# A two-model forward pass of fp32 on one core: S5 preparation in 25 smaller steps, residuals loaded by tile, packed matmuls in SSD and S5, and VectorE's stage steps ahead of the low part of the weights

## The chip, the cores and the metric

The kernel runs on one core of one Trainium2 chip. The metric is the device time of one execution in microseconds (us), as the median of several runs; smaller is better. A profiled execution is one run with the hardware profiler on, and its own time is given beside its span.

## What is computed

Two models follow each other on one sequence of 512 tokens and width 2048, everything in fp32. The first has a layer of gated linear attention (4 heads) and forgetting attention (8 heads), and a layer with an S5 state space model and a gated linear unit. The second has two equal layers with three branches each: SSD (Mamba-2 in chunks of 128, 16 heads of 64), a conformer convolution with 31 taps, and differential attention (4 heads). Around each stand RMS norms, a wide input projection and an output projection onto the residual. Cut to what the change touches:

```python
# S5: x_t = Lbar x_{t-1} + Bbar u_t ; y_t = Re(C x_t) + D u_t, 128 groups of 16 channels, 64 complex states each
bu = einsum('gpc,blgc->blgp', bb, uf); x = associative_scan(...); y = einsum('gcp,blgp->blgc', c, x) + d * uf
# SSD, one head h, chunks of L = 128:
a_cs = jnp.cumsum(a, axis=-1)
decay_in = segsum_exp(a_cs)                       # exp(a_cs[l] - a_cs[s]) for s <= l
y_diag = jnp.einsum("bcgls,bcgjls,bcsgjp->bclgjp", cb, decay_in, xdt)
y = (y_diag + y_off + d_skip * x) * silu(z)
x = x + jnp.einsum("bse,ed->bsd", y_all, w_out[l])
```

## The kernel before, in words

**Projections.** All dense products are cut into 528 units (`UNITS`). A unit is one load of 512 KB of weights and 24 matmuls of 128x128 by 128x512: each fp32 product is made of three fp32r products, high by high, low by high and high by low part (`unit_pe`, L541 and L542). Eight units (or six and two, for output projections that are split into `x_in`/`x_normed` and `x_part`) make a pass, which fills four PSUM banks. The last unit of a pass goes bank by bank, so that the banks are emptied (`evac_dve`, `evac_act`) while it still runs; the first unit of the next pass waits for each bank to be free.

**Slots.** Each engine runs through the same 528 slots in order. In slot t TensorE does unit t and then the steps of that slot that belong to the small computations between the projections ("stages": GLA, forgetting attention, S5, SSD, convolution, attention). Their steps are Python generators, one `yield` for each slot, placed by hand in tables (`stage`, `place`); `take(t)` issues those of slot t. Four PSUM banks (`mid`) are theirs.

**Weights.** The SyncE queue (SP) loads unit t+5 in slot t (`weights_sp`) once VectorE (DVE) has made the low part of unit t+2 (a ring of three buffers). In slot t ScalarE (ACT) rounds unit t+2 to its high part (`weights_act`, L394), once unit t-1 is used up, and DVE then subtracts to get the low part (`weights_dve`, L467).

**Activations.** Sixteen tiles of 128x512 for each projection phase are split into high and low parts too ("conversions", two tiles a slot as a rule, at slots listed in `conversions()`): a load (`convert_sp`, four buffers), ACT's high part, and for some phases squares for the norm that GpSimd (POOL) adds up (`convert_act`, `add_pool`), and DVE's low part (`convert_dve`, L525 and L528). They lie in slots -1 to 4, 106 to 111, 140 to 147, 202 to 209, 234 to 239 with 242 and 243, 266 to 271 with 274 and 275, 362 to 365 with 368 and 369, 396 to 403, 490 to 493 with 496 and 497, and one tile at a time in slots 117, 121, 125, 129, 213 and in the attention heads of the last two layers.

**The order on the two queues.** This is what the change turns on; VectorE (L2637 to L2648) and SP (L2572 to L2582), for each slot t:

```python
# vector
evac_dve(e, ENDS[t - 1])          # if slot t-1 ended a pass
weights_dve(e, t + AHEAD)         # low part of unit t+2
convert_dve(e, n)                 # conversions of slot t
take(t)                           # stage steps of slot t
# sync
store_sp(e, ENDS[t - 1]); take(t)
weights_sp(e, t + 5)              # waits for the low part of unit t+2
residual_sp(e, UNITS[t][0])       # in the first slot of a pass that adds a residual
convert_sp(e, n)                  # loads for the conversions of slot t+1
```

**Parts that the change touches.** `prep_dve` (L760 to L856) computes the S5 constants in 12 steps in slots 5 to 16. `sw_pe` (L988) makes the S5 kernels of 8 groups by matmuls with 16 output rows, into rows 0 to 15 of two banks, for each of 16 tiles in slots 76 to 138. In SSD each head h starts in slot 48+h of its layer (the layers start at slots 272 and 400): ACT spreads `a` (L1897), TensorE makes the cumulated sums with 4 fp32 matmuls (L1934), DVE and ACT form the exponentials (L1958, L1902, L1905), DVE multiplies (L1963), and two slots after its start TensorE makes y with 4 fp32 matmuls of 64 output rows (L1943), even heads in rows 0 to 63 of a bank and odd heads in rows 64 to 127. A residual of 4 tiles (1 MB) is loaded by one DMA (`residual_sp`, L347) in the first slot of its pass, after the pass before has been emptied, and added at L514.

Of the kernel before, what the change touches and what calls it, by code (L numbers as in the profile page):

```python
# [177 lines left out]
def build(nc, I, X):  # L178

    with ExitStack() as ctx:  # L180
# [38 lines left out]
        SMO = sb("small_out", [P, L])  # L219
        ONES = sb("ones", [P, P])  # L220
# [6 lines left out]
        ARENA_N = 19920  # L227
# [29 lines left out]
        out_stored, xr_in, zr_in = sem("out_stored"), sem("xr_in"), sem("zr_in")  # L257
# [38 lines left out]
        def x_source(q):  # L296

            w, l = PASSES[q], LAYER[q]
            if w.kind == "x_in":
                return I["x"][:, 4 * w.index:4 * w.index + 4, :], None  # L300
            if w.kind == "x_part":
                return XPART[l][4 * w.index:4 * w.index + 4].rearrange("k p n -> p k n"), q - 4
            src = XS[l - 1]
            return src[4 * w.index:4 * w.index + 4].rearrange("k p n -> p k n"), X_PASS[l - 1] + w.index
# [19 lines left out]
        def residual_sp(e, q):  # L324
# [8 lines left out]
            if PASSES[q].kind == "glu":  # L333
                i = PASSES[q].index
                stored(e, FIRST_GATE + i)
                e.dma_start(XR[:, :, :], FMD[1][4 * i:4 * i + 4].rearrange("k p n -> p k n")).then_inc(xr_in, 16)
                if i == 0:
                    for x in ZR_FREE:
                        e.wait_ge(*x)
                for k in range(4 * i, 4 * i + 4):  # L340
                    e.wait_ge(*mix_stored(3, k))
                e.dma_start(ZR[:, :, :], MX[3][4 * i:4 * i + 4].rearrange("k p n -> p k n")).then_inc(zr_in, 16)
                return
            src, by = x_source(q)
# [24 lines left out]
        def store_sp(e, q):  # L369
# [7 lines left out]
            for s in range(4):  # L377
# [9 lines left out]
                e.dma_start(dst, OUTB[:, s, :]).then_inc(out_stored, 16)  # L387

# [81 lines left out]
        def evac_dve(e, q):  # L470
# [26 lines left out]
            elif w.kind == "glu":  # L497
                e.wait_ge(xr_in, 16 * (XR_TURN[q] + 1))
                e.wait_ge(zr_in, 16 * (w.index + 1))
                for s in range(4):  # L500
                    e.wait_ge(*FREE[q, s])
# [3 lines left out]
            else:  # L505
                e.wait_ge(xr_in, 16 * (XR_TURN[q] + 1))
                if w.kind == "x_normed":
                    for s in range(4):
                        k = 4 * w.index + s
# [172 lines left out]
        def small_act(e, ph):  # L682
# [4 lines left out]
            if i == 1:  # L687
                e.wait_ge(*fx_p.at("lc", 7))
# [72 lines left out]
        def prep_dve(e):  # L761
# [72 lines left out]
            for d in range(8):  # L834
                if d % 3 == 0:
                    yield
# [1923 lines left out]
```

## Time and profile before

| | |
|---|---|
| median of 3 runs | 3628.29 us (3622.89 to 3630.3) |
| profiled execution, its own time | 3625.47 us |
| its span | 3623.7 us |
| granted TensorE clock, mean | 0.982 |
| TensorE busy | 3464.2 us, 96% |
| TensorE weight loads busy | 2770.9 us, 76% |
| VectorE busy | 2127.2 us, 59% |
| ScalarE busy | 1288.7 us, 36% |
| GpSimd busy | 150.4 us, 4% |
| DMA | 574.58 MB, mean 159 GB/s |

All times in the rows are us from the first instruction of the span, durations of groups of instructions in us or, where it is said, ns. Matmuls overlap: a 128x512 matmul is shown with about 390 ns although the next one starts earlier, so their starts, not their lengths, tell the pace.

### The profile page before, as it was taken

The page shows a single profiled execution, that of the slowest core. Times are in us where ns is not written, and L with a number is a line of the kernel's source. Part 1 is how long each engine was busy: PE and PEld are TensorE (multiplying, and loading weights), DVE is VectorE, ACT ScalarE, POOL GpSimd, SP SyncE. Part 2 cuts the span into 40 slices and gives each one's busy share as a digit, 9 for nine tenths or more (in the row PEclk, how much of TensorE's full clock was granted, in tenths as well). Part 3 has the DMA queues.
Part 4 walks back from the last instruction along what each step waited for, and adds up shares of the span by engine and source line. Part 5 has one row for each costly group of instructions (what it writes and reads, how often), then busy time and mean ns, then how long its engine had stood idle before and what let it go on. Part 6 is the DMA issues. An engine that isn't in the chain of part 4 may idle for free.

```text
span 3623.7 us, 42976 instructions
## 1 busy us (share of the span) xinstructions
PE 3464.2 (96%) x15890; PEld 2770.9 (76%) x15890; DVE 2127.2 (59%) x3122; ACT 1288.7 (36%) x2013; POOL 150.4 (4%) x100
## 2 busy tenths in 40 slices
PE   8899999999999999999989999998999999999899
PEld 6687887777777888788878876776777887677677
DVE  6755546677655645434244775566755476565774
ACT  4233324444332233423152224324423223532442
POOL 2000000000020000000050000000002000000000
PEclk9899999999999999999999999998999999999899
DMA  4233335566665555645443442344446343334445
GB/s 163 100 123 123 112 130 180 175 235 217 227 212 183 177 176 185 202 168 198 152 161 117 164 137 99 114 139 164 151 160 216 106 166 132 104 122 161 141 156 198
DMA packets 286129, 574.58 MB, mean 159 GB/s; under 512 B 61392, under 2 KB 101088, under 8 KB 285408
## 3 DMA queue, kind: packets, MB, share of 16 engines
q1 hardware_dynamic: 285920, 571.83, 47.0%
q8 instruction: 127, 2.08, 0.2%
q14 instruction: 82, 0.67, 0.1%
HBM read 440.65 MB, written 131.07 MB: 158 GB/s over the span
## 4 chain that ended last, share of the span: by engine, by line
PE 52%; issue 23%; DVE 13%; ACT 6%; DMA 3%; DVEq 2%; POOLq 1%; SPq 0%; ACTq 0%
PE bank L542 34%; PE bank L541 11%; DVE weights_low L467 3%; ACT weights_high L394 2%; DVE arena L1963 2%; ACT arena L1905 1%; POOLq L453 1%; DVE residual_in L2037 1%; DVE arena L1958 1%; DMA convert_in<-x 1%; PE bank L1076 1%; DVEq L2541 1%; ACT arena L1902 1%; DVE act_low L525 1%; PE bank L988 1%
## 5 line engine op out<-in xcount | busy, mean ns | idle before, releaser
L542 PE MATMUL bank<-act_high,weights_high 128*128 128x512 f32 x3584 | 1449.3, 404 | 77.1 <-DVE stream_out L514 34.7
L542 PE MATMUL bank<-act_low,weights_high 128*128 128x512 f32 x3584 | 1416.8, 395 | 0.0
L467 DVE TENSOR_TENSOR weights_low<-weights_raw,weights_high 128x1024 fp32r<-128x1024 f32 x528 | 656.9, 1244 | 1122.0 <-ACT weights_high L394 1119.4
L394 ACT ACTIVATE weights_high<-weights_raw 128x1024 fp32r<-128x1024 f32 x528 | 558.1, 1057 | 1517.7 <-PE bank L542 1256.4
L542 PE MATMUL bank<-act_high,weights_low 128*128 128x512 f32 x3584 | 962.8, 389 | 0.0
L542 PEld LDWEIGHTS bank<-act_high,weights_high 128*128 128x128 f32 x3584 | 686.1, 191 | 248.0 <-issue 54.4
L542 PEld LDWEIGHTS bank<-act_low,weights_high 128*128 128x128 f32 x3584 | 685.7, 191 | 138.5 <-issue 2.9
L542 PEld LDWEIGHTS bank<-act_high,weights_low 128*128 128x128 f32 x3584 | 672.8, 188 | 140.1
L541 PE MATMUL bank<-weights_high,act_high 128*128 128x512 f32 x640 | 255.4, 399 | 23.3 <-DVE stream_out L480 18.1
L541 PE MATMUL bank<-weights_high,act_low 128*128 128x512 f32 x640 | 250.6, 392 | 0.0
L2037 DVE SCALAR_TENSOR_TENSOR residual_in<-residual_in,arena 128x512 f32<-128x512 f32 x240 | 180.4, 752 | 20.8 <-issue 1.8
L541 PE MATMUL bank<-weights_low,act_high 128*128 128x512 f32 x640 | 169.5, 389 | 0.0
L541 PEld LDWEIGHTS bank<-weights_high,act_high 128*128 128x128 f32 x640 | 121.0, 189 | 52.4 <-issue 27.3
L541 PEld LDWEIGHTS bank<-weights_high,act_low 128*128 128x128 f32 x640 | 121.0, 189 | 24.9 <-issue 0.7
L541 PEld LDWEIGHTS bank<-weights_low,act_high 128*128 128x128 f32 x640 | 120.1, 188 | 25.0
L452 POOL TENSOR_TENSOR square_sum<-square_sum,squares 128x512 f32<-128x512 f32 x74 | 118.1, 1597 | 323.7 <-ACT squares L442 317.6
L450 POOL COPY square_sum<-squares 128x512 f32<-128x512 f32 x6 | 6.6, 1095 | 2740.6 <-ACT squares L442 2740.6
L525 DVE SCALAR_TENSOR_TENSOR act_low<-convert_in,norm_gains,act_high 128x512 fp32r<-128x512 f32 x64 | 81.5, 1301 | 38.3 <-ACT act_high L433 38.2
L514 DVE TENSOR_TENSOR stream_out<-bank,residual_in 128x512 f32<-128x512 f32 x112 | 71.1, 684 | 32.1 <-DMA residual_in<-x_part 17.4
L1943 PE MATMUL bank<-arena 128*64 128x512 f32 (+3 forms) x256 | 77.9, 448 | 10.9 <-DVE arena L1963 10.9
L1902 ACT ACTIVATE arena<-arena 128x128 f32<-128x128 f32 x128 | 29.1, 298 | 151.1 <-DVE arena L1958 151.1
L480 DVE TENSOR_TENSOR stream_out<-bank,scale_bcast 128x512 f32<-128x512 f32 x116 | 73.3, 685 | 11.1 <-PE bank L542 7.9
(318 smaller groups left out, 2879.4 us busy)
## 6 DMA issues: line engine op xcount, KB each, us to landing
weights_raw<-in_w_all SPq DMA_DIRECT2D x528, 512.0 KB, 3.3
convert_in<-mix SPq DMA_DIRECT2D x80, 256.0 KB, 4.2
fm_b<-stream_out SPq DMA_DIRECT2D x72, 256.0 KB, 2.3
mix<-arena SPq DMA_DIRECT2D x64, 256.0 KB, 2.7
x_part<-stream_out SPq DMA_DIRECT2D x48, 256.0 KB, 2.2
residual_in<-x_part SPq DMA_DIRECT2D x12, 1024.0 KB, 7.0
x<-stream_out SPq DMA_DIRECT2D x48, 256.0 KB, 2.6
convert_in<-x SPq DMA_DIRECT2D x48, 256.0 KB, 3.9
```

Of the source, the lines that this page charges most:

```text
L394: e.activation(WH[:, t % 3, :], RAW[:, t % 3, :], ACT.Copy).then_inc(wh_ready, 1)
L452: e.tensor_tensor(acc, acc, SQ[:, n % 2, :], ALU.add).then_inc(sq_added, 1)
L467: e.tensor_tensor(WL[:, t % 3, :], RAW[:, t % 3, :], WH[:, t % 3, :].bitcast(F32), ALU.subtract).then_inc(wl_ready, 1)
L480: e.tensor_tensor(OUTB[:, s, :], bank[s][:, :], RF[:, :], ALU.mult).then_inc(evac_v, 1)
L514: e.tensor_tensor(OUTB[:, s, :], bank[s][:, :], XR[:, s, :], ALU.add).then_inc(evac_v, 1)
L525: e.scalar_tensor_tensor(HL[:, k, :], x, GAIN[:, GAIN_OF[ph], k:k + 1], hi, ALU.mult, ALU.subtract).then_inc(conv_lo, 1)
L541: return e.matmul(bank[s][:, :], h[:, s * P:(s + 1) * P], a, start=start, stop=stop)
L542: return e.matmul(bank[s][:, :], a[:, s * P:(s + 1) * P], h, start=start, stop=stop)
L1902: e.activation(packed(ee, b, 0, 1), packed(ee, b, 0, 1), ACT.Exp)
L1943: mm = e.matmul(mid[2 + k % 2][r, b * P:], sd_xdt[:, b, h * 64:(h + 1) * 64], packed(sd_e[h % 2], b), start=b == 0, stop=b == TB - 1)
L1963: e.tensor_tensor(sd_e[h % 2], sd_e[h % 2], sd_cb[h // 8], ALU.mult).then_inc(*sd_dm.mark("m"))
L2037: ins = e.scalar_tensor_tensor(cf_acc, u[:, k:k + L], w[:, k:k + 1], cf_acc, m, add)
```

## The change

It has five parts.

1. `prep`: the same operations in 25 steps, in slots 10 to 21, 29 to 32, 43 to 45, 56 to 58, 69 to 71, 74 and 75. Its data moves in the arena so that GLA no longer waits for it.
2. Residuals: four semaphores in place of one. Where a pass that adds a residual follows another such pass, tile s is loaded right after tile s of the pass before has been stored.
3. S5 kernels: 32 output rows in place of 16 for each group, group g into rows 32*(g%4) of one bank; one ACT copy in place of two; the diagonal added on all partitions.
4. SSD: the cumulated sums of a head come from one fp32r matmul (a one-hot `SMW[:, h, :]`, spread once by ACT, times `ROWS_R`, which holds the rounded sums of all heads and what rounding left), so L1897 and L1934 go; 4 fp32 matmuls and 3 DVE operations are added once per layer. y is made for two heads at a time, alternately in rows 0 to 63 and 64 to 127, one slot later.
5. VectorE's order in a slot: conversions, stage steps, then the low part of the weights.

```diff
-        def residual_sp(e, q):
+        def residual_free_sp(e, q):
...
+        def residual_sp(e, q, s):
...
-            e.dma_start(XR[:, :, :], src).then_inc(xr_in, 16)
+            e.dma_start(XR[:, s, :], src).then_inc(xr_in[s], 16)
+        def follows(q):
+            return q in XR_TURN and q - 1 in XR_TURN
...
                 e.dma_start(dst, OUTB[:, s, :]).then_inc(out_stored, 16)
+                if follows(q + 1):
+                    residual_sp(e, q + 1, s)
...
                 for s in range(4):
                     wait_acc(e, q, s)
+                    e.wait_ge(xr_in[s], 16 * (XR_TURN[q] + 1))
                     e.tensor_tensor(OUTB[:, s, :], bank[s][:, :], XR[:, s, :], ALU.add).then_inc(evac_v, 1)
...
-        PREP_STEPS = 12
+        PREP_SLOTS = [*range(10, 22), *range(29, 33), *range(43, 46), *range(56, 59), 69, 70, 71, 74, 75]
+        PREP_STEPS = len(PREP_SLOTS)
...
             for g in range(S5_G):
-                mm = e.matmul(mid[2 + g // 4][0:S5_C, (g % 4) * P:(g % 4 + 1) * P], sw_vb[:, g, P - S5_C:],
+                r = slice(32 * (g % 4), 32 * (g % 4) + 32)
+                mm = e.matmul(mid[2][r, (g // 4) * P:(g // 4 + 1) * P], sw_vb[:, g, P - 2 * S5_C:],
                               sw_cp[:, g, 0:P], start=True, stop=True)
...
         def ssd_pe(e, l, h):
...
-            for b in range(TB):
-                mm = e.matmul(mid[h % 2][:, b * P:(b + 1) * P], sd_ab[h % 2][:, b, :], TRI[:, :], start=True, stop=True)
-            mm.then_inc(*sd_pacs.mark("acs"))
-            yield
-            yield
-            e.wait_ge(*sd_dm.at("m", t))
-            if k >= 2:
-                e.wait_ge(*sd_yd.at("y", l * 8 + k - 2))
-            r = slice(64 * (h % 2), 64 * (h % 2) + 64)
-            for b in range(TB):
-                mm = e.matmul(mid[2 + k % 2][r, b * P:], sd_xdt[:, b, h * 64:(h + 1) * 64], packed(sd_e[h % 2], b),
-                              start=b == 0, stop=b == TB - 1)
-            mm.then_inc(*sd_py.mark("y"))
+            e.matmul(mid[h % 2][:, :], SMW[:, h, :], ROWS_R[:, :], start=True, stop=True).then_inc(*sd_pacs.mark("acs"))
+            yield
+            yield
+            yield
+            if h % 2:
+                e.wait_ge(*sd_dm.at("m", t))
+                if k >= 2:
+                    e.wait_ge(*sd_yd.at("y", l * 8 + k - 2))
+                for b in range(TB):
+                    for n in (h - 1, h):
+                        r = slice(64 * (n % 2), 64 * (n % 2) + 64)
+                        mm = e.matmul(mid[2 + k % 2][r, b * P:], sd_xdt[:, b, n * 64:(n + 1) * 64], packed(sd_e[n % 4], b),
+                                      start=b == 0, stop=b == TB - 1)
+                mm.then_inc(*sd_py.mark("y"))
...
                 if t - 1 in ENDS:
                     evac_dve(e, ENDS[t - 1])
-                if t + AHEAD < NU:
-                    weights_dve(e, t + AHEAD)
                 for n in BY_SLOT.get(t, ()):
                     convert_dve(e, n)
                 take(t)
+                if t + AHEAD < NU:
+                    weights_dve(e, t + AHEAD)
```

## Rows read from the trace of the kernel before

**Rows 1.** The page: busy time by engine, and the chain that ended last.
```profile
PE 3464.2 (96%) x15890; PEld 2770.9 (76%) x15890; DVE 2127.2 (59%) x3122; ACT 1288.7 (36%) x2013; POOL 150.4 (4%) x100
PE 52%; issue 23%; DVE 13%; ACT 6%; DMA 3%; DVEq 2%; POOLq 1%; SPq 0%; ACTq 0%
```

**Rows 2.** Stretches: slots 212-261, both SSD stretches, slots 362-366 (busy, clock, DMA, GB/s).
```profile
1527.10:1799.10 272.00, 272.00 (x1202) 225.30 (x1201) 97.61 (x107) 74.70 (x84) 0.00 (x0) 1.00 0.50 171
2156.10:2320.90 164.80, 156.60 (x690) 111.50 (x688) 86.59 (x124) 82.05 (x219) 11.99 (x7) 0.98 0.34 115
3043.80:3208.20 164.40, 153.72 (x690) 110.20 (x688) 86.24 (x123) 81.72 (x218) 11.98 (x7) 1.00 0.34 116
2463.20:2518.50 55.30, 39.75 (x158) 29.39 (x157) 39.50 (x70) 23.84 (x38) 0.00 (x0) 0.81 0.32 109
```

**Rows 3.** TensorE's timeline: start, length, operation, count [idle before].
```profile
1408.40 0.39 PE L542 MATMUL bank<-act_high,weights_high 128*128 128x512 f32 x1
1408.63 0.40 PE L542 MATMUL bank<-act_low,weights_high 128*128 128x512 f32 x1
...
2219.36 2.37 PE L1943 MATMUL bank<-arena 128*64 128x512 f32 x8
2221.66 1.16 PE L1934 MATMUL bank<-tri,arena 128*128 128x128 f32 x8
...
3482.53 0.92 PE L2245 MATMUL bank<-arena 64*128 64x384 f32 x4
...
634.20 1.92 PE L988 MATMUL bank<-arena 128*16 128x128 f32 x16
```

**Rows 4.** DVE's and TensorE's timeline at the pass ends of slots 7, 15 and 311.
```profile
62.59 0.54 PE L542 MATMUL bank<-act_high,weights_high 128*128 128x512 f32 x1 [3.38 <-DVE stream_out L482]
...
132.72 2.48 DVE L480 TENSOR_TENSOR stream_out<-bank,scale_bcast 128x512 f32<-128x512 f32 x4
133.56 0.77 PE L541 MATMUL bank<-weights_high,act_high 128*128 128x512 f32 x1 [18.07 <-DVE stream_out L480]
...
2105.44 2.48 DVE L480 TENSOR_TENSOR stream_out<-bank,scale_bcast 128x512 f32<-128x512 f32 x4
2106.28 0.47 PE L542 MATMUL bank<-act_high,weights_high 128*128 128x512 f32 x1 [3.50 <-DVE stream_out L480]
```

**Rows 5.** DVE's timeline, the residual of slot 139's pass.
```profile
998.87 2.48 DVE L514 TENSOR_TENSOR stream_out<-bank,residual_in 128x512 f32<-128x512 f32 x4 [3.66 <-DMA residual_in<-x_part]
```

**Rows 6.** DVE, SP and ACT timelines, slots 234 and 235: from low part to conversion.
```profile
1648.09 1.23 DVE L467 TENSOR_TENSOR weights_low<-weights_raw,weights_high 128x1024 fp32r<-128x1024 f32 x1 [4.21 <-ACT weights_high L394]
1649.35 0.33 SPq L322 DMA_DIRECT2D weights_raw<-in_w_all  x1
1649.77 0.86 SPq L367 DMA_DIRECT2D convert_in<-mix  x2
1654.31 1.27 ACT L435 ACTIVATE act_high<-convert_in 128x512 fp32r<-128x512 f32 x2 [0.36 <-DMA convert_in<-mix]
1655.13 1.28 DVE L528 TENSOR_TENSOR act_low<-convert_in,act_high 128x512 fp32r<-128x512 f32 x2
```

**Rows 7.** DVE's timeline in slots 107 and 108: conversion, then stage steps.
```profile
759.71 1.29 DVE L528 TENSOR_TENSOR act_low<-convert_in,act_high 128x512 fp32r<-128x512 f32 x2
...
764.23 1.23 DVE L918 TENSOR_TENSOR arena<-arena 128x1024 f32<-128x1024 f32 x1
766.08 1.23 DVE L467 TENSOR_TENSOR weights_low<-weights_raw,weights_high 128x1024 fp32r<-128x1024 f32 x1 [0.62 <-ACT weights_high L394]
```

**Rows 8.** DVE's and TensorE's timeline in slots 270 to 272 (conversions with squares).
```profile
1849.24 2.04 DVE L467 TENSOR_TENSOR weights_low<-weights_raw,weights_high 128x1024 fp32r<-128x1024 f32 x1 [0.20 <-ACT weights_high L394]
1851.60 1.38 DVE L525 SCALAR_TENSOR_TENSOR act_low<-convert_in,norm_gains,act_high 128x512 fp32r<-128x512 f32 x1 [0.32 <-ACT act_high L433]
1855.52 0.75 DVE L525 SCALAR_TENSOR_TENSOR act_low<-convert_in,norm_gains,act_high 128x512 fp32r<-128x512 f32 x1 [2.54 <-ACT act_high L433]
1864.16 0.77 PE L542 MATMUL bank<-act_high,weights_high 128*128 128x512 f32 x1 [10.54 <-DVE stream_out L514]
```

More of the change, by code:

```diff
@@ L1659, in build @@
         sd_mx = [sem(f"sd_mix{n}") for n in range(2)]
-        sd_tp, sd_ta, sd_td = steps("sd_dt_pe", "dt sums"), steps("sd_dt_act", "ln"), steps("sd_dt_dve", "pad y a tot bias")
+        sd_tp, sd_ta, sd_td = steps("sd_dt_pe", "dt sums"), steps("sd_dt_act", "ln pick"), steps("sd_dt_dve", "pad y a tot rows")
         sd_cp, sd_ca, sd_cd = steps("sd_conv_pe", "xt"), steps("sd_conv_act", "silu"), steps("sd_conv_dve", "conv")
@@ L1675, in build @@
         sd_e = [A(PACK[4]) for _ in range(2)]
-        sd_ab = [A(TB, P) for _ in range(2)]
         sd_x, sd_z, sd_y = A(2, L), A(2, L), A(2, L)
@@ L1680, in build @@
         sd_w, sd_dsk, sd_pick = A(12, 5), A(8), A(16)
+        after_conv = Arena(0, 6 * L)
+        sd_e += [after_conv(PACK[4]) for _ in range(2)]
+        sd_two = sd_x[:, 0, :].rearrange("p (b n) -> p b n", b=TB)
         conv = Arena(SD_E, SD_E + 2 * PACK[4])
@@ L1710, in ssd_pre_pe @@
             e.matmul(mid[0][:, 0:64], TRI[:, :], a2, start=True, stop=True)
-            e.matmul(mid[0][:, 64:128], ONES[:, :], a2, start=True, stop=True).then_inc(*sd_tp.mark("sums"))
+            e.matmul(mid[0][:, 64:128], ONES[:, :], a2, start=True, stop=True)
+            for b in range(TB):
+                mm = e.matmul(mid[1][:, b * P:(b + 1) * P], sd_two[:, b, :], TRI[:, :], start=True, stop=True)
+            mm.then_inc(*sd_tp.mark("sums"))
             yield
@@ L1761, in ssd_pre_dve @@
                 e.drain()
-            e.drain().then_inc(*sd_td.mark("bias"))
+            e.tensor_copy(ROWS_R[:, :], mid[1][:, :])
+            e.drain()
+            low = slice(64, P)
+            e.tensor_tensor(ROWS_R[low, :], mid[1][low, :], ROWS_R[low, :].bitcast(F32), ALU.subtract)
+            e.drain().then_inc(*sd_td.mark("rows"))
             yield
@@ L1887, in ssd_sp @@
             yield
+            yield
             if h % 2:
@@ L1953, in ssd_dve @@
             e.wait_ge(*sd_pacs.at("acs", t))
-            ee, ps = sd_e[h % 2], mid[h % 2]
-            if h >= 2:
-                e.wait_ge(*sd_py.at("y", t - 2))
+            ee, ps = sd_e[h % 4], mid[h % 2]
+            if h >= 4:
+                e.wait_ge(*sd_py.at("y", l * 8 + k - 2))
+            if h == 2:
+                for n in range(2):
+                    e.wait_ge(sd_xst[n], 16 * (l * 4 + 4))
             for b in range(TB):
@@ L2485, in build @@
         add_stat(0, STAT[0])
-        stage("prep", place(5, PREP_STEPS), sp=prep_sp, act=prep_act, dve=prep_dve)
+        stage("prep", PREP_SLOTS, sp=prep_sp, act=prep_act, dve=prep_dve)
         for h in range(4):
@@ L2577, in _ @@
                     weights_sp(e, t + 5)
-                if UNITS[t][0] in XR_TURN and FIRST[UNITS[t][0]] == t:
-                    residual_sp(e, UNITS[t][0])
+                q = UNITS[t][0]
+                if q in XR_TURN and FIRST[q] == t and not follows(q):
+                    residual_free_sp(e, q)
+                    for s in range(4):
+                        residual_sp(e, q, s)
                 for n in BY_SLOT.get(t + 1, ()):
```

132 lines of the change are left out of this document (75 added, 57 removed).

## The prediction

> **What bounds the kernel now.** I read the page first. TensorE is busy for 96% of the span and holds half of the chain that ended last [rows 1]: whatever shortens its work counts in full, and whatever delays it too. Then the stretches. Slots 212 to 261 have only projection units: 50 slots in 272.0 us, TensorE never idle, at full clock, so a unit costs 5.44 us [rows 2], 24 matmuls that start 0.23 us apart [rows 3]. 528 units make 2872 us; the other 750 us of the span are stage matmuls and stalls. The two SSD stretches of 18 slots take 164.8 and 164.4 us, 9.1 us a slot, of which 5.44 is the unit [rows 2]. Last the timelines at pass ends: there TensorE waits for DVE to empty the banks, 18.07 us at slot 15, 3.38 at slot 7, 3.50 at slot 311 [rows 4] and 10.54 at slot 271 [rows 8]. DVE is only 59% busy, but it works in order, and when a pass ends while it has a backlog, TensorE pays for that.
>
> **SSD (part 4).** The 8 instructions of the sums (4 fp32 matmuls are two each) take 1.16 us a head, those of y 2.37 us [rows 3]. One fp32r matmul at 0.23 replaces the first. For y, two heads work in different columns of the array. The trace has no such pair, but one in different rows: 4 instructions of 384 columns in 0.92 us, while y's 8 instructions, 2560 columns, take 2.37 us, so 1536 columns in turn would take 1.4: they run side by side [rows 3]. I take the same here: a pair costs what one head did. A stretch is then 18 x 5.44 + 16 x 0.23 + 8 x 2.4 = 121 us, with 3 us for what stays of waits 124, which is 41 and 40 us less [rows 2]: 81 us. ACT loses a spread per head and DVE gains three operations per layer, both beside slots of some 6.9 us. TensorE gains 4 small matmuls per layer, 1.2 us each time. Without packing, 8 x 2.37 x 2 = 38 us of this is missing; more than 81 + 6 us can't come, since 118 us are pure matmuls. Taken: 80.
>
> The Trainium skill speaks both ways on this: TensorEngine Tiling (Array Packing), Tiling Modes, lets different tiles load and multiply in parallel, while TensorE: Matmul & The Clock Gate, Part 3, says that a weight load overlaps matmuls in flight only if its row group differs, and column pairs share theirs. By the first the term is as above, by the second it tends to the 38 us less; no row here decides.
>
> **S5 kernels (part 3).** 16 instructions take 1.92 us [rows 3], in 16 tiles 31 us. In four columns groups at once it would be a quarter, -23 us; with no packing 0, plus nothing for 32 rows. The pair of rows 3 shows two at once, not four: I take half, 0.95 us, -15.
>
> **Prep (part 1).** The 18.07 us before slot 16 and some 2 us of half-speed matmuls behind it (0.77 us where 0.39 to 0.47 is usual), and the 3.38 us at slot 7 with as much again, all come from prep steps ahead of the evacuation [rows 4]. Spread over 25 slots of 2 us each they lie in DVE's idle time, save around slot 20: -24. It could be -18 if GLA's slots come under pressure.
>
> **Residuals (part 2).** DVE waited 3.66 us for the 1 MB load at slot 139's pass end [rows 5]; three or four more such waits cost TensorE about 1 us each. Tile by tile, and issued when the store is, the load is there in time: -4 (0 to -10).
>
> **The order on DVE, where it helps (part 5).** At slot 311 the convolution steps run first and the banks are emptied at 2105.44, while TensorE waits 3.50 us [rows 4]; with the clock's fall it is 5.6. These steps wait for nothing. Placed ahead of the low part, which waits for ACT, they fill DVE's idle time. Such ends are at slots 311, 439 and, 1.5 to 2 us each, six others: -22. In S5 slots the stage step comes late itself and the low part now lies behind it, ahead of the evacuation: +1.2 at four ends, which I set against some relief in attention.
>
> **The order on DVE, where it hurts.** The low part of unit t+2 is what SP waits for in slot t, and behind that wait on SP's queue stand the loads for the conversions of slot t+1. Now the low part is made first, so loads are on their way while DVE converts slot t. After the change it is made last, so every conversion slot is a closed chain: low part, load, ACT's high part, DVE's conversion, stage steps, low part. Its length [rows 6]: the low part ends at 1649.32, the loads are issued at 1649.77 and ACT can't start before 1654.31; its two high parts end at 1655.58, DVE's second low part 0.7 later: 7.0 us; with the low part of 1.23 us it is 8.2 us, and the stage steps come on top. That is against 5.44 to 6.5 us on TensorE. The lateness adds up slot by slot until a pass ends, and there TensorE pays all of it beyond about 1 us:
> - slots 234 to 239: 5 x (8.2 - 5.44) = 14 us, now nothing;
> - slots 106 to 111: stage steps of 2.2 to 4.5 us (761.0 to 765.5) [rows 7], 11.6 against 6.3 us, five times, and 2 us at the start: 28 us, now nothing; the single tiles of slots 117, 125 and 129, each 6 us behind its low part, 5, 2 and 5 us: 40 in all;
> - slots 202 to 209: the same with stage steps in four slots: 22 us at slot 208, of which 6 are there now: 16;
> - slots 266 to 271: squares paced by POOL hold the second conversion 4 us behind the first [rows 8]; load 5, first high part 1.9, second conversion's end 4.7 behind, low part: 12 us. Six slots make 72 us, so 37 over the units' 33 (the excess is 13 now); 24, and 5 more at slots 274 to 276, where the norm waits for the last squares: 29;
> - slots 140 to 147 and 396 to 403: 9.1 us a slot with squares, a pass end every second slot, 10 us each: 20;
> - slots 362 to 365 and 490 to 493: TensorE already waits for DVE here (55.3 us for 5 slots, clock 0.81 [rows 2]); three load waits of 4.7 us enter DVE's chain, less what it idles now, 12 us, and 4 for the two pairs behind: 32;
> - slots 0 to 4: three tiles a slot, 10 us a slot; the first norm is ready 14 us later: 14.
> Sum 165 us. Behind the longer gaps TensorE runs at the lower clock for a while, as after 133.56 [rows 4]: 6 us more. Bounds: the units' slack (low parts are made two slots ahead) might hide a half, 80 us; with waits of 7 us for loads (beside stores) it is 230.
>
> **Sum.** -80 - 15 - 24 - 4 - 22 = -145; +165 + 6 = +171: +26 us on the profiled execution's own 3625.5, so 3651; the median shown is 2.8 us above that execution, about a hundredth of what is in doubt here, and I give 3650.
>
> **Rivals.**
> - *Conversions stay cheap* (faster, 0.33). If the loads come back sooner, or the two slots of low parts in hand absorb the lateness, the closed chain costs half: 3651 - 85 = 3566; not at all, 3480. It decides if a conversion slot on DVE stays under about 7 us instead of 8.2 and more. For it: DVE catches up 4 us a slot behind each run, and runs that end away from a pass end can use slack. Against it: at six of the runs a pass ends inside or right behind, and 1654.31 is a landing, not a guess.
> - *Columns don't pack* (0.12). The row pair is no proof for columns, and both use the same rows. Then 38 + 15 us are missing: 3704.
> - *Gains and losses meet* (0.07): each side is off by 20 us; 3625.
> - *The forecast* (0.48): 3650, its own range 3610 to 3690.
>
> A measurement of this kernel can tell about 0.2%, 7 us, from no change. Faster takes in the first rival and the lower tail of the forecast's, 0.37; same 0.08; slower 0.55. The range for 8 in 10 leaves out the free case at the bottom and the sum of both bad ones at the top: 3560 to 3715.
>
> **What would show it.** Right: SSD stretches of about 124 us, with pairs of L1943's successor in 2.4 us; no 18 us gap at slot 15; in conversion slots DVE idle 5 us before each conversion with the load as the reason, conversions 8 to 12 us apart, and TensorE idle for 10 to 30 us at the pass ends of slots 111, 207, 239 and 271, on DVE's evacuation (ACT's at 239). Wrong: those four gaps below 5 us (first rival), or an SSD stretch of 140 us (second). A conversion slot of 8 us with no gap at pass ends would mean that the slack is larger than I read.

## The result, and the profile after

The changed kernel takes 3695.05 us in the median of 4 runs (3692.54 to 3699.61), against 3629.3 us (3622.89 to 3630.74) before: ratio 1.0186, interval 1.0168 to 1.0204, 66 us slower. The forecast was 3650 us. Its sign was right and the range 3560 to 3715 held the time, but the loss is three times the forecast's 22 us.

The page of the changed kernel, answering to [rows 1]:

```profile
span 3694.5 us, 42715 instructions
PE 3423.4 (93%) x15682; PEld 2749.5 (74%) x15682; DVE 2114.4 (57%) x3132; ACT 1266.8 (34%) x1967; POOL 135.6 (4%) x100
```

TensorE does 41 us less work in a span that is 71 us longer: its idle time went from 159 to 271 us. Next the stretches, each from the first instruction of a slot to that of another, so that all waits are in. "Forecast" is the loss or gain that the prediction gave the place.

| slots | before | changed | difference | forecast |
|---|---|---|---|---|
| 0 to 6 | 42.2 | 58.5 | +16.3 | +14 |
| 7 to 19 (part 1) | 104.9 | 79.2 | -25.7 | -24 |
| 106 to 111 | 40.4 | 68.0 | +27.6 | +28 |
| 112 to 131 | 154.9 | 167.3 | +12.4 | +12 |
| 139 to 151 | 84.5 | 100.0 | +15.5 | +10 |
| 202 to 209 | 62.1 | 86.1 | +24.0 | +16 |
| 234 to 241 | 43.6 | 57.4 | +13.8 | +14 |
| 266 to 271 | 43.4 | 70.0 | +26.6 | +24 |
| 272 to 277 | 38.6 | 49.5 | +10.9 | +5 |
| 319 to 339 and 447 to 467 (SSD) | 362.3 | 282.0 | -80.3 | -80 |
| 294 to 318, 345 to 361, 439 to 446, 473 to 489 | 406.8 | 391.2 | -15.6 | -22 |
| 362 to 371 and 490 to 499 | 183.5 | 216.3 | +32.8 | +32 |
| 396 to 407 | 85.2 | 102.5 | +17.3 | +10 |

Four of these stretches in the changed kernel (slots 234 to 241, 266 to 271, 106 to 111, 202 to 209; the columns are those of [rows 2]):

```profile
1711.70:1769.10 57.40, 46.84 (x193) 37.92 (x192) 22.37 (x28) 17.76 (x24) 0.00 (x0) 0.91 0.49 171
1899.70:1969.70 70.00, 37.24 (x145) 29.20 (x143) 23.02 (x20) 29.47 (x43) 33.51 (x24) 0.78 0.24 82
732.80:800.80 68.00, 43.06 (x200) 33.57 (x198) 34.32 (x44) 21.38 (x34) 0.00 (x0) 0.81 0.45 151
1492.50:1578.60 86.10, 62.50 (x299) 51.73 (x298) 38.94 (x49) 29.48 (x43) 0.00 (x0) 0.85 0.48 157
```

No engine is the bound: at slots 266 to 271 TensorE is busy for 37 of 70 us, VectorE for 23, ScalarE for 29, GpSimd (POOL) for 34, the DMA engines for a quarter. All wait for each other. The closed chain can be read link by link in slots 235 to 237 of the changed kernel, from the timelines of VectorE, ScalarE and SP (answering to [rows 6]):

```profile
1719.36 0.86 SPq L374 DMA_DIRECT2D convert_in<-mix  x2
1723.03 1.22 ACT L444 ACTIVATE act_high<-convert_in 128x512 fp32r<-128x512 f32 x2 [4.58 <-DMA convert_in<-mix]
1723.70 1.29 DVE L538 TENSOR_TENSOR act_low<-convert_in,act_high 128x512 fp32r<-128x512 f32 x2 [4.79 <-ACT act_high L444]
1724.91 1.22 DVE L476 TENSOR_TENSOR weights_low<-weights_raw,weights_high 128x1024 fp32r<-128x1024 f32 x1
1726.15 0.33 SPq L323 DMA_DIRECT2D weights_raw<-in_w_all  x1
1726.58 0.86 SPq L374 DMA_DIRECT2D convert_in<-mix  x2
1731.78 1.27 ACT L444 ACTIVATE act_high<-convert_in 128x512 fp32r<-128x512 f32 x2 [6.58 <-DMA convert_in<-mix]
1732.45 1.33 DVE L538 TENSOR_TENSOR act_low<-convert_in,act_high 128x512 fp32r<-128x512 f32 x2 [6.32 <-ACT act_high L444]
1733.69 1.22 DVE L476 TENSOR_TENSOR weights_low<-weights_raw,weights_high 128x1024 fp32r<-128x1024 f32 x1
```

The low part ends at 1726.13, SP's wait ends, the loads go out at 1726.58, the tile is there at 1731.78, the conversion and the next low part end at 1734.91: 8.8 us for this turn and 7.2 for the one before, where the forecast said 8.2 and a unit takes 5.44. With squares the low parts of slots 269 to 271 start at 1929.83, 1942.02 and 1954.30, 12.2 us apart (forecast 12). TensorE pays at the pass ends, and also inside passes, where a stage matmul waits. From its timeline, slots 240, 272, 276 and 109 of the changed kernel:

```profile
1755.34 0.76 PE L552 MATMUL bank<-act_high,weights_high 128*128 128x512 f32 x1 [7.35 <-DVE act_low L538]
...
1969.75 0.77 PE L552 MATMUL bank<-act_high,weights_high 128*128 128x512 f32 x1 [17.47 <-DVE stream_out L524]
...
2006.78 1.87 PE L616 MATMUL bank<-ones,square_sum 128*128 128x1 f32 x8 [8.07 <-POOL arena L461]
...
776.74 1.08 PE L1003 MATMUL bank<-arena 128*32 128x128 f32 x16 [13.61 <-ACT arena L972]
```

The gap at slot 272 was 10.54 us [rows 8]; the others were not there. The last two are places the forecast priced low or not at all: a norm that waits for POOL to add the last squares, and an S5 kernel whose input is copied by ScalarE behind a late conversion. The four pass ends that the prediction named for gaps of 10 to 30 us (slots 111, 207, 239 and 271) have gaps of 7.49, 11.15, 7.35 and 17.47 us. The loss of 27.6 us at slots 106 to 111 came out as forecast, but about half of it is paid in slot 109 and not at the pass end.

Over the places of loss in the table, with slots 152 to 201 and 210 to 233 (5.0 and 2.4 us, no forecast), the span grew by 205 us: TensorE's idle time by 163 us and its busy time by 42. All other slots together gained 134 us.

TensorE's matmuls in the places of the gains, of the changed kernel (y of a pair of heads, a head's sums, S5 kernels), answering to [rows 3]:

```profile
2295.10 2.37 PE L1979 MATMUL bank<-arena 128*64 128x512 f32 x16
2297.40 0.50 PE L1968 MATMUL bank<-rows_rounded,small_weights 128*128 128x512 f32 x1
...
702.34 0.65 PE L1003 MATMUL bank<-arena 128*32 128x128 f32 x16
```

A pair of heads costs the 2.37 us that one head did, as forecast. The 16 instructions of S5 kernels fell from 1.92 to 0.65 us, more than the 0.95 forecast.

### The profile page after: what moved, and what is told of

Read it like the earlier page. It is cut to its first block, busy times and chain, and to the rows that moved or that the text cites. A ratio compares the mean times of both kernels' runs of the same rounds, so it can differ in the third digit from the quotient of the medians.

```text
span 3694.5 us, 42715 instructions
## 1 busy us (share of the span) xinstructions
PE 3423.4 (93%) x15682; PEld 2749.5 (74%) x15682; DVE 2114.4 (57%) x3132; ACT 1266.8 (34%) x1967; POOL 135.6 (4%) x100
## 4 chain that ended last, share of the span: by engine, by line
issue 63%; PE 30%; POOLq 3%; DVE 2%; DMA 1%; ACT 0%; DVEq 0%; SPq 0%; ACTq 0%
PE bank L552 22%; PE bank L551 5%; POOLq L462 3%; PE bank L1979 1%; DMA convert_in<-mix 1%; PE bank L728 0%; PE bank L2285 0%; PE bank L616 0%; PE bank L1884 0%; DVE weights_low L476 0%; PE bank L1968 0%; PE bank L2317 0%; PE bank L1844 0%; PE bank L2286 0%; DVE arena L2002 0%
## 5 line engine op out<-in xcount | busy, mean ns | idle before, releaser
L552 PE MATMUL bank<-act_low,weights_high 128*128 128x512 f32 x3584 | 1431.7, 399 | 0.0
L552 PEld LDWEIGHTS bank<-act_high,weights_high 128*128 128x128 f32 x3584 | 697.2, 195 | 300.8 <-issue 126.0
L552 PEld LDWEIGHTS bank<-act_low,weights_high 128*128 128x128 f32 x3584 | 696.4, 194 | 143.8 <-issue 2.9
L538 DVE TENSOR_TENSOR act_low<-convert_in,act_high 128x512 fp32r<-128x512 f32 x80 | 54.8, 692 | 202.0 <-ACT act_high L444 189.4
L551 PE MATMUL bank<-weights_low,act_high 128*128 128x512 f32 x640 | 169.6, 389 | 0.0
L461 POOL TENSOR_TENSOR square_sum<-square_sum,squares 128x512 f32<-128x512 f32 x74 | 105.7, 1429 | 360.6 <-ACT squares L451 356.1
L444 ACT ACTIVATE act_high<-convert_in 128x512 fp32r<-128x512 f32 x64 | 40.3, 631 | 183.6 <-DMA convert_in<-mix 183.2
L451 ACT ACTIVATE squares<-convert_in 128x512 f32<-128x512 f32 x64 | 40.0, 625 | 145.3 <-DMA convert_in<-x 120.3
L1641 DVE TENSOR_TENSOR arena<-bank,arena 128x512 f32<-128x512 f32 x16 | 11.1, 692 | 133.0 <-ACT arena L1600 133.0
```

What stands on the lines that cost most here:

```text
L444: e.activation(HH[:, k, :], x, ACT.Copy).then_inc(conv_hi, 1)
L451: e.activation(SQ[:, n % 2, :], x, ACT.Square, scale=scale).then_inc(sq_ready, 1)
L461: e.tensor_tensor(acc, acc, SQ[:, n % 2, :], ALU.add).then_inc(sq_added, 1)
L538: e.tensor_tensor(HL[:, k, :], x, hi, ALU.subtract).then_inc(conv_lo, 1)
L551: return e.matmul(bank[s][:, :], h[:, s * P:(s + 1) * P], a, start=start, stop=stop)
L552: return e.matmul(bank[s][:, :], a[:, s * P:(s + 1) * P], h, start=start, stop=stop)
```

## The experiments

Eleven kernels, in the order in which they ran. In each, "base" is the kernel that the edit starts from.

**e1_low_first.** Base: changed kernel, VectorE's order put back.

```diff
+                if t + AHEAD < NU:
+                    weights_dve(e, t + AHEAD)
                 for n in BY_SLOT.get(t, ()):
                     convert_dve(e, n)
                 take(t)
-                if t + AHEAD < NU:
-                    weights_dve(e, t + AHEAD)
```

> The changed kernel with VectorE's order alone put back (low part of the weights, conversions, stage steps); parts 1 to 4 stay. Closed-chain theory (all that the conversion slots lose, 215 us summed over the slots between the two traces, comes from the low part standing last; the order gives 17 us at other pass ends): all of the 215 goes and the 17 comes back, 3480 to 3510 us, ratio to the kernel before 0.959 to 0.967; TensorE's idle gaps at the pass ends of slots 111, 207, 239 and 271 fall from 7.5, 11.2, 7.4 and 8.7 us to under 5 us; SSD stretches stay at 141 us for slots 319 to 340. Rival (a good part of the loss comes from parts 1 to 4, such as S5 steps of the preparation in slots with other work, the 32-row kernels or the later heads): 3560 us or more.

Measured: 3558.98 us (3554.99 to 3563.41), ratio 0.9809 (0.9794 to 0.9825). All of the losses went, stretch by stretch (slots 234 to 241 43.5 us, 266 to 271 43.4, 202 to 209 62.4), so VectorE's order is their cause and parts 1 to 4 are not; that it works through the wait on SP's queue is shown by e3. The total lies above the theory's range and just below the rival's bound, because the SSD stretches grew. They take 168.9 us each in place of 141.0. The stretch in e1 and in the changed kernel:

```profile
2108.90:2277.80 168.90, 144.05 (x650) 108.14 (x650) 93.96 (x136) 76.39 (x207) 12.20 (x7) 0.94 0.37 126
```

```profile
2260.80:2401.80 141.00, 140.17 (x651) 104.60 (x650) 91.44 (x140) 76.81 (x207) 9.86 (x7) 1.00 0.45 151
```

So the old order has a closed chain of its own in SSD. ScalarE's and VectorE's timelines in e1, slots 334 and 335:

```profile
2232.40 1.08 ACT L403 ACTIVATE weights_high<-weights_raw 128x1024 fp32r<-128x1024 f32 x1
...
2238.57 0.91 ACT L1934 ACTIVATE arena<-arena 128x128 f32<-128x128 f32 x4 [4.55 <-DVE arena L1997]
2239.38 1.63 ACT L1937 ACTIVATE arena<-bank,arena 128x128 f32<-128x128 f32 x6
2240.88 1.08 ACT L403 ACTIVATE weights_high<-weights_raw 128x1024 fp32r<-128x1024 f32 x1
```

```profile
2233.52 1.23 DVE L476 TENSOR_TENSOR weights_low<-weights_raw,weights_high 128x1024 fp32r<-128x1024 f32 x1 [3.46 <-ACT weights_high L403]
2234.97 2.27 DVE L2002 TENSOR_TENSOR arena<-arena 128x1280 f32<-128x1280 f32 x1 [0.23 <-issue]
2237.41 1.12 DVE L1997 TENSOR_SCALAR arena<-bank,arena 128x128 f32<-128x128 f32 x4 [0.16 <-issue]
2241.99 1.23 DVE L476 TENSOR_TENSOR weights_low<-weights_raw,weights_high 128x1024 fp32r<-128x1024 f32 x1 [3.46 <-ACT weights_high L403]
```

High part on ScalarE (to 2233.48), low part on VectorE, its stage steps, ScalarE's exponentials, which wait for them, and then ScalarE's next high part: 8.47 us per turn here and 9.43 in every second slot (the low part before starts at 2224.09). Before the change TensorE's own slot was 8.9 us, so this chain nearly hid; with slots of 5.7 and 8.2 us it is the bound.

**e2_before_low_last.** Base: the kernel before, with VectorE's order changed as in part 5 and nothing else.

> The kernel before with VectorE's order alone changed (conversions, stage steps, low part). Closed-chain theory: the loss comes whole without parts 1 to 4: 3629 + 215 - 17 = 3827, range 3800 to 3850; slots 234 to 241 take 57 us (43.6 before), slots 266 to 271 70 us (43.4). Rival (the loss needs the other parts, or the other parts make it dearer): 3700 to 3760.

Measured: 3810.15 us (3807.12 to 3820.27), ratio 1.0508 (1.0486 to 1.0529). The total lies in the theory's range, and the losses need no other part: slots 234 to 241 take 57.0 us, 266 to 271 69.5. It has the matmuls of the kernel before, so the two pages show how the 185 us of span divide (e2's page; before, TensorE was busy for 3464.2 of 3623.7 us [rows 1]):

```profile
span 3808.5 us, 42976 instructions
PE 3501.9 (92%) x15890; PEld 2800.6 (74%) x15890; DVE 2110.1 (55%) x3122; ACT 1291.0 (34%) x2013; POOL 133.8 (4%) x100
```

147 us are idle time of TensorE and 38 us the same 15890 matmuls taking longer, with a mean granted clock of 0.96 against 0.982.

**e3_sp_loads_first.** Base: changed kernel. VectorE's new order stays; on SP's queue the conversions' loads go ahead of the weights' wait.

```diff
                 take(t)
+                for n in BY_SLOT.get(t + 1, ()):
+                    convert_sp(e, n)
                 if t + 5 < NU:
                     weights_sp(e, t + 5)
...
-                for n in BY_SLOT.get(t + 1, ()):
-                    convert_sp(e, n)
```

> The changed kernel, VectorE's new order kept, but on the SP queue the loads for the conversions of slot t+1 are issued before the load of weight unit t+5 and its wait for the low part of unit t+2. Theory that the loss is the wait on SP's queue (low part, then load, then conversion): the chain is open, conversions find their tile loaded, DVE waits of 5 us before a conversion go; slots 234 to 241 back at 44 us, whole kernel 3470 to 3500. Rival (it is the low part's late place on VectorE itself that stalls TensorE, wherever the loads are issued): less than half of the 215 us comes back, 3590 or more.

Measured: 3481.77 us (3478.39 to 3485.28), ratio 0.9596 (0.9582 to 0.9611). No instruction was added or taken away and VectorE kept the order that costs 182 us in e2; 213 us are gone. The wait was on SP's queue. The page of e3 has the same 15682 matmuls as that of the changed kernel:

```profile
span 3480.1 us, 42715 instructions
PE 3373.5 (97%) x15682; PEld 2715.6 (78%) x15682; DVE 2112.4 (61%) x3132; ACT 1263.5 (36%) x1967; POOL 143.3 (4%) x100
```

The closed chain thus costs 214 us of span: 164 us of idle time of TensorE, and 50 us by which the same matmuls take longer, at a mean granted clock of 0.961 against 0.986. VectorE's timeline in e3, the same slots as above, and the stretches of slots 234 to 241 and 266 to 271:

```profile
1624.00 1.29 DVE L538 TENSOR_TENSOR act_low<-convert_in,act_high 128x512 fp32r<-128x512 f32 x2 [3.00 <-ACT act_high L444]
1625.21 1.22 DVE L476 TENSOR_TENSOR weights_low<-weights_raw,weights_high 128x1024 fp32r<-128x1024 f32 x1
1629.44 1.29 DVE L538 TENSOR_TENSOR act_low<-convert_in,act_high 128x512 fp32r<-128x512 f32 x2 [3.01 <-ACT act_high L444]
```

```profile
1611.30:1654.80 43.50, 43.50 (x194) 36.02 (x193) 22.19 (x28) 17.47 (x24) 0.00 (x0) 1.00 0.65 224
1785.30:1830.00 44.70, 34.69 (x146) 27.96 (x144) 25.88 (x20) 29.37 (x43) 36.58 (x24) 0.91 0.33 117
```

VectorE still waits 3 us before a conversion, but the turns are 5.44 us apart: TensorE's pace, with no idle time in 43.5 us. The largest loss left is at slots 202 to 209, which take 68.5 us, against 62.1 before the change.

**e4_low_in_middle.** Base: changed kernel; VectorE's order is conversions, low part, stage steps.

> The changed kernel with VectorE's order conversions, low part, stage steps. Closed-chain theory: the load is still behind the low part, so what has no stage steps in its conversion slots keeps its loss: slots 234 to 241 stay at 57 us, slots 266 to 271 at 70 us; where stage steps of 2 to 4.5 us stood in the chain the loss falls: slots 106 to 111 from 68 to about 53 us, slots 202 to 209 from 86 to about 74; the gain at slots 311 and 439 (5 us each) goes. Sum about 3695 - 15 - 12 + 14 = 3680, range 3660 to 3690. Rival (conversions ahead of the low part cost nothing, the stage steps ahead of it do): slots 234 to 241 back at 44 us, 3600 or less.

Measured: 3674.07 us (3668.46 to 3676.25), ratio 1.0124 (1.0109 to 1.0139). The rival is out: slots 234 to 241 and 266 to 271 keep their loss. In e4, slots 106 to 111, 234 to 241 and 266 to 271:

```profile
735.50:783.00 47.50, 38.24 (x199) 30.23 (x197) 33.15 (x43) 21.39 (x34) 0.00 (x0) 1.00 0.63 214
1653.80:1710.10 56.30, 46.84 (x194) 37.93 (x193) 22.32 (x28) 17.71 (x24) 0.00 (x0) 0.91 0.51 174
1840.60:1910.60 70.00, 37.43 (x145) 29.30 (x144) 23.04 (x20) 29.46 (x43) 33.50 (x24) 0.78 0.23 82
```

Stage steps in the chain cost 20 us at slots 106 to 111 (expected 15) and 17 at slots 202 to 209 (expected 12); where there are none, their place changes next to nothing. The price of the chain itself is the load. That the total fell into the range expected is luck: nobody expected the SSD stretches to grow from 141.0 to 169.3 and 168.8 us, 56 us in all, and about as much came back at slots 112 to 131, 362 to 371 and 490 to 499 (17 us each), which had no term either. The SSD stretches take what they take in e1. Common to both is the low part ahead of the stage steps, which bears out the second chain.

**e5_low_by_slot.** Base: changed kernel, SP's queue as in it; the low part is first only in slots with conversions in them or in the next.

```diff
+                early = t in BY_SLOT or t + 1 in BY_SLOT
+                if early:
+                    weights_dve(e, t + AHEAD)
                 for n in BY_SLOT.get(t, ()):
                     convert_dve(e, n)
                 take(t)
-                if t + AHEAD < NU:
+                if not early and t + AHEAD < NU:
                     weights_dve(e, t + AHEAD)
```

> The changed kernel, SP's queue as in it, but VectorE makes the low part first where this slot or the next has conversions, and last in all other slots. Closed-chain theory: it matters only in those slots that the low part stands ahead, so it does as well as opening the chain on SP's queue (3481.8): 3475 to 3495, with slots 234 to 241 at 44 us, slots 266 to 271 at 43, the SSD slots 319 to 340 at 141 us. Rival (the late low part also costs in slots without conversions, or the order must be the same throughout): above 3510.

Measured: 3483.69 us (3483.07 to 3488.95), ratio 0.9606 (0.959 to 0.9622). The chain can be opened at either link. By stretches it beats e3 at slots 202 to 209 (61.5 against 68.6 us) and 106 to 111 (39.2 against 41.4) and loses at slots 362 to 366 (55.2 against 49.2) and 490 to 494 (55.9 against 51.4).

**e6_issue_order.** Base: e3. Only the order in which packed matmuls are issued changes.

```diff
-                for b in range(TB):
-                    for n in (h - 1, h):
+                for n in (h - 1, h):
+                    for b in range(TB):
...
-            for g in range(S5_G):
+            for g in (0, 4, 1, 5, 2, 6, 3, 7):
```

> Base is e3 (changed kernel, loads of conversions first on SP; 3481.8 us). Only the order in which packed matmuls are issued is changed: y of a pair of heads one head after the other (4 and 4) in place of alternately, and the 8 S5 groups so that neighbours share their columns (0, 4, 1, 5, 2, 6, 3, 7). Theory that columns work side by side only if neighbouring instructions are in different ones: a pair of heads takes 4.7 us instead of 2.37, +19 us per layer (slots 319 to 340 from 141 to 160 us), and S5's 16 instructions 1.3 us instead of 0.65, +10 us in all; sum 3520 to 3535. Rival (the 2.37 us for a pair comes from something else, shorter reading of 64 rows or fewer waits, and not from working side by side; or the order does not matter): 3482, within 5 us.

Measured: 3509.74 us (3503.27 to 3520.08), ratio 0.9676 (0.9656 to 0.9697). A pair of heads, e6's TensorE timeline:

```profile
2145.80 3.93 PE L1979 MATMUL bank<-arena 128*64 128x512 f32 x16
```

3.93 us against 2.37, where two heads one after the other would be 4.74: the same instructions with the same data are 1.55 us slower a pair, 25 us in all. The single instructions in the traces show why. In the changed kernel the first matmuls of the two heads start 7 ns apart, and so does each pair after them: they run side by side. In e6 the first head's eight instructions come first; the second head's first one starts 1.56 us after the first head's, next to its fifth, and needs its own 2.37 us from there: 3.93. So the saving is work side by side, and most of it hangs on neighbours in different columns. S5's order made next to no difference (slots 97 and 100 take 6.11 and 6.20 us in e3, 6.13 and 6.23 in e6): the 16 instructions take 0.65 us in e3 and 0.67 in e6, in both cases they start in fours, the first four within 20 ns in e3 and within 40 ns in e6. It fits that in e6 four instructions in a row share a column group, and do not hold the next group back, while the eight of a head did until the fifth. Only half of the theory held.

**e7_residual_at_start.** Base: e3, part 2 undone in its place in time.

```diff
         def follows(q):
-            return q in XR_TURN and q - 1 in XR_TURN
+            return False
```

> Base is e3 (3481.8 us). The residual's four tiles are all loaded in the first slot of their pass again, as before the change (still four loads with a semaphore each). Theory of the prediction: tile-by-tile loading behind the stores is worth 4 us, 0 to 10: 3486. Rival (the loads were in time anyhow, or crowd the stores): 3482 or less, within the error.

Measured: 3473.68 us (3470.19 to 3477.09), ratio 0.9574 (0.956 to 0.9589). This is the rival's side, and beyond it: with SP's queue open, part 2 costs 8 us, of which 5.5 lie at slots 139 to 147 and 3.3 at slots 396 to 403. SP's timeline at the pass end of slot 139, in e3 and in e7:

```profile
952.38 0.42 SPq L394 DMA_DIRECT2D x<-stream_out  x1
952.84 0.43 SPq L351 DMA_DIRECT2D residual_in<-x_part  x1
...
957.45 0.47 SPq L351 DMA_DIRECT2D residual_in<-x_part  x1
958.02 0.94 SPq L374 DMA_DIRECT2D convert_in<-x  x2
```

```profile
952.56 2.31 SPq L394 DMA_DIRECT2D x<-stream_out  x4
954.96 1.03 SPq L374 DMA_DIRECT2D convert_in<-x  x2
```

In e3 the four residual tiles stand ahead of the conversions' loads, which go out 3 us later; VectorE then waits 4.94 us for that conversion in e3 and 2.25 in e7.

**e8_prep_in_12.** Base: e3, all preparation steps back in slots 5 to 16.

> Base is e3 (3481.8 us). All steps of the S5 preparation are put back into slots 5 to 16. Theory: the 26 us that slots 7 to 16 gained between the two traces come back, 3505 to 3512, with a TensorE gap of some 18 us at the end of slot 15. Rival (VectorE's new order, with the emptying of banks and the stage steps ahead of the low part, covers the long steps): less than 10 us, 3482 to 3492.

Measured: 3511.74 us (3510.64 to 3513.86), ratio 0.968 (0.9665 to 0.9694): 30 us, with this gap at the end of slot 15 in e8 (18.07 us before [rows 4]):

```profile
136.95 0.76 PE L551 MATMUL bank<-weights_high,act_high 128*128 128x512 f32 x1 [14.71 <-DVE stream_out L489]
```

The theory held: VectorE's order doesn't cover the steps, and spreading them gains 30 us. 26 of the 30 us lie in slots 7 to 19.

**e9_best.** Base: e7, and VectorE's low part first in five ranges of slots.

```diff
+                early = any(a <= t < b for a, b in ((105, 112), (139, 148), (202, 209), (265, 272), (395, 404)))
+                if early:
+                    weights_dve(e, t + AHEAD)
...
-                if t + AHEAD < NU:
+                if not early and t + AHEAD < NU:
```

> Base is e7 (loads of conversions first on SP, residuals at the start of their pass; 3473.7 us). VectorE makes the low part first in slots 105 to 111, 139 to 147, 202 to 208, 265 to 271 and 395 to 403 alone, and last elsewhere. From e5, where the same order gave 7.1 us at slots 202 to 209, 2.2 at 106 to 111, 1.4 at 266 to 271 and 1 to 1.5 at 396 to 403, and cost 3 us at slots 125 to 131 and 6 and 4.5 at slots 362 to 366 and 490 to 494, which keep the low part last here: 3461 to 3466. Rival (the gains of e5 were made up by its queue order, or are scattered back behind): 3472 or more.

Measured: 3457.33 us (3455.71 to 3458.86), ratio 0.953 (0.9516 to 0.9544): 170 us faster than before and 238 faster than the change, the best version found. The 16 us over e7 are a little more than expected: slots 202 to 209 gave 5.8, 396 to 403 4.0, 106 to 111 3.1.

```profile
span 3456.4 us, 42752 instructions
PE 3365.8 (97%) x15682; PEld 2708.2 (78%) x15682; DVE 2121.0 (61%) x3132; ACT 1262.9 (37%) x1967; POOL 152.3 (4%) x100
```

**e10_before_two_orders.** Base: e2, with e3's edit to SP's queue.

> The kernel before with VectorE's new order and the loads of conversions first on SP: part 5 alone with its chain open. Theory that order and SSD part work on each other (with the old matmuls an SSD stretch gains 12 us from either alone, 40 from both): 3578 to 3592 (12 a stretch, 5 at slots 311 and 439, 10 at the attention heads, 6 elsewhere). Rival (the gains add up: all parts together 3482, parts 1 to 4 alone 3559, so the order alone is worth 77 us): 3545 to 3560.

Measured: 3578.55 us (3573.62 to 3579.47), ratio 0.9865 (0.9848 to 0.9881). The total lies at the lower end of the theory's range. With the chain open the order is worth 49 us on the old matmuls and 77 on the new ones (3558.98 to 3481.77): the two work on each other, in the SSD stretches (169.6 and 169.9 us here, 169.0 and 169.2 in e1, 141 with both).

**e11_residual_alone_undone.** Base: changed kernel, with e7's edit.

> The changed kernel with part 2 alone undone: the residual's tiles are all loaded in the first slot of their pass. In e3 and e7, with SP's queue open, part 2 costs 8 us. In the closed chain the load at the start of the pass stands behind SP's wait for the low part: e2, which has no part 2, takes 74.5 us for slots 139 to 147 and 67.7 for slots 396 to 403, the changed kernel 67.1 and 61.2. Theory that part 2's worth hangs on what it is queued behind: here undoing it costs 10 to 14 us, 3705 to 3709. Rival (part 2 costs in itself, by loads that crowd the conversions' loads): undoing it gains some 8 us, 3687.

Measured: 3716.15 us (3715.2 to 3718.6), ratio 1.0248 (1.0231 to 1.0265). In the changed kernel part 2 gains 21 us, more than the 10 to 14 expected (slots 139 to 147 take 74.3 against 67.1 us, 396 to 403 68.9 against 61.2, and some 3 us each lie at slots 106 to 111, 112 to 131 and 362 to 371). SP's timeline in TensorE's slot 141, in the changed kernel and in e11:

```profile
1024.22 0.33 SPq L323 DMA_DIRECT2D weights_raw<-in_w_all  x1
1024.65 0.85 SPq L374 DMA_DIRECT2D convert_in<-x  x2
```

```profile
1031.30 0.33 SPq L323 DMA_DIRECT2D weights_raw<-in_w_all  x1
1031.73 1.80 SPq L351 DMA_DIRECT2D residual_in<-x_part  x4
1033.63 0.85 SPq L374 DMA_DIRECT2D convert_in<-x  x2
```

In e11 the residual's four loads are a link of the closed chain: they stand between SP's wait for the low part and the conversions' loads. Between this low part and the next conversion VectorE waits 8.87 us in e11 and 5.24 in the changed kernel. VectorE's waits for the residual itself are 6.0 us in all in e11, so they are the smaller part of the 21. With the queue open part 2 costs 8 us. In both cases what counts is whether the residual's loads stand ahead of the conversions' loads, and behind which wait.

## Why the prediction was right, and where it failed

**Right.** The mechanism and its price per turn (8.2 us forecast, 7.2 and 8.8 measured). The closed chain was named link by link, and e3 shows it: one move on SP's queue takes 213 us away. The rival "conversions stay cheap" fell: the low parts in hand did not hide a half of the waiting; slots 234 to 241 have 10.6 us more idle time, where five late turns had been priced at 14, and 3.3 us of slower matmuls. Prep came out at -25.7 for -24. The rival "columns don't pack" fell by e6: the two heads' matmuls start 7 ns apart, and issued head by head a pair takes 1.55 us more. The Trainium skill's sentence that a weight load overlaps matmuls in flight only if its row group differs (TensorE: Matmul & The Clock Gate, Part 3), read as the prediction read it, would have left y at some 4.7 us a pair. The trace disagrees with it: both heads use all 128 rows, and the second head's weight load starts 5 ns behind the first head's matmul. By the Trainium skill's TensorEngine Tiling (Array Packing), Tiling Modes, different tiles load and multiply in parallel; with that the trace agrees.

**Failed: the term for the clock, 6 us.** It came from one row, the matmuls behind 133.56 [rows 4], while every other term of "The order on DVE, where it hurts" was worked out as waiting. The runs show that the waiting was right in sum and the clock was not. In the places of loss TensorE's idle time grew by 163 us, for a sum of 165; its busy time grew by 42 us, for a term of 6. The changed kernel and e3 have the same matmuls, and there the difference is 164 us idle and 50 us busy (the 42 are less because the S5 kernels in slots 106 to 131 became shorter). Together that is 205 us of loss for 171. The other 11 us of the 45 by which the span's difference, 71 us, exceeds the 26 forecast are gains of 134 us for 145, and some 8 us of them are those S5 kernels again.

**Partly luck: that the waiting sums to 165.** Errors at single places cancel:
- *The end of a norm.* Behind the squares TensorE waits for POOL's last sum. The prediction had 5 us at slots 274 to 276, and 8 us of idle time came there; 6 at slots 148 to 151 and 7 at slots 404 to 407 had no term. With the slower matmuls behind them, these three places lost 10.9, 9.3 and 10.2 us.
- *Slots 202 to 209*: 20 us for 16. The lateness was counted only up to the evacuation in slot 208; TensorE's stage matmuls of slots 205 and 209 also wait, 6.15 and 4.14 us, for ScalarE's stage steps, which stand behind conversions there.
- *Less*: 12 us for 20 at slots 139 to 147 and 396 to 403, 9 for 14 at slots 0 to 6, and some 3 less each at slots 106 to 111 and 234 to 241.

**Failed: adding the parts as if each stood alone.** Parts 1 to 4 alone gain 69 us (e1), where 145 - 22 = 123 was forecast, since the SSD stretches give 24 us and not 80 without the new order. The prediction said that ACT's and DVE's work lies "beside slots of some 6.9 us" and did not follow the chain of high part, low part, stage steps and exponentials, 8.5 to 9.4 us. The SSD term came out, -80.3 for -80, only because part 5 opens this chain, which the prediction did not count on. The new order alone costs 182 us (e2), where 171 - 22 = 149 was forecast. Both single figures were thus too favourable, by 54 and 33 us, 87 together. The two singles add up to +114; together it is +66. Of the 48 us between them, 33 lie in the two SSD stretches, and 13 at slots 139 to 147 and 396 to 403, where part 2 softens the closed chain (e11). This joint effect hid about half of the two errors.

**Failed: residuals.** -4 was set, between 0 and -10, with a loss excluded. It is -21 in the changed kernel and +8 with SP's queue open. What stands behind the four tiles on SP's queue, the conversions' loads, was not asked.

**S5 kernels** were undersized: 1.27 us of TensorE's work in each of 16 tiles, 20 us, for 15. Four column groups do work at once, where the prediction took half of that effect. **Order where it helps**: 16 us for 22 at pass ends outside SSD.

The forecast's own range, 3610 to 3690, missed the time by 5 us. The 36 us missing from the clock's term use up nearly all of the 40 us that it had above 3650, and its higher figure for the losses, 230 us, came from longer waits for loads and not from the clock.

Some counts ahead of the result are off. The preparation's list of slots has 27 entries, not 25. Part 4 adds five VectorE operations a layer, not three (the pages count 3122 and 3132). In the prediction the pure matmuls of an SSD stretch, "118 us", are 121 by its own terms, and 72 us at slots 266 to 271 are 39 over the units' 33, not 37; neither changes the forecast by more than 2 us. What stays open: which of the changed kernel's gaps brings how much of the 50 us of slower matmuls; only the sum was measured.

## What to carry to other kernels

When an operation moves later on one engine, follow it onto every queue where something waits for it, and look at what stands behind that wait: here a load that had nothing to do with the low part was queued behind it, and a free reordering cost 182 us. Prefetches go ahead of waits on a queue, not behind them; once they do, the same reordering gains 49 to 77 us. And test parts in the company in which they will run: a shorter slot on the bounding engine exposes chains between the others, and the sign of a part can change with its place in a queue. Price a wait twice, once as idle time and once as slower matmuls behind it: here 164 us of the one brought 50 of the other.

## What the hardware showed that was not expected

- Column-packed fp32 matmuls of two heads took 2.37 us a pair when issued alternately and 3.93 when issued head by head, where one after the other with nothing side by side would be 4.74. In the second order the next head's first instruction, the ninth issued, started next to the fifth. The 8 groups of 32 output rows, 16 instructions of 128 columns, took 0.65 us with neighbours in different column groups and 0.67 with four in a row in the same one.
- Waits cost a second time through the clock: with unchanged matmuls, 147 us of added idle time came with 38 us of added busy time, at a granted mean of 0.96 against 0.982 (e2 against before), and 164 us came with 50, at 0.961 against 0.986 (changed kernel against e3). Behind the gaps of 7.35 and 17.47 us the first matmuls are shown with 0.76 and 0.77 us, against 0.39 at full clock, that is at 1.2 in place of 2.4 GHz, and the next ones start 0.43 us apart in place of 0.23.
